# Low parts of the turned attention tiles taken by VectorE out of the transposes' bank

## What is computed

```
q, k = partial_rope(rmsnorm(q, q_gain)), partial_rope(rmsnorm(k, k_gain))   # two maps per head, 64 wide
s = einsum('mbhqd,mbhkd->mbhqk', q_blk, k) / sqrt(64)
p = softmax(s);  a = p[0] - lam * p[1]                # 8 heads, 4 blocks of 128 queries
o = einsum('bhqk,bhkv->bhqv', a, v)                   # v 128 wide
o = rmsnorm(o, sub_gain) * (1 - lambda_init)
x = x + o @ w_o
```

## Time and profile before

| | |
|---|---|
| median of 3 runs | 1055.51 us (1054.57 to 1055.61) |
| span of the profiled execution | 1052.2 us, first to last instruction |
| what lies around the span | 3.3 us, if the profiled execution took the median |
| TensorE busy | 1010.8 us, 96% |
| VectorE busy | 603.8 us, 57% |
| ScalarE busy | 410.5 us, 39% |
| GpSimd busy | 278.8 us, 26% |
| mean granted TensorE clock | 0.994 of full speed |

### The profile page before, as it was taken

The page is one execution under the profiler, slowest core; times in us unless marked ns, Lnnn a source line. Parts: engine busy times, 40 slices in busy tenths (PEclk is TensorE's granted clock), DMA queues, the critical chain, the costliest instruction groups (busy, mean ns, idle before and its releaser), DMA issues.

```text
span 1052.2 us, 13519 instructions
## 1 busy us (share of the span) xinstructions
PE 1010.8 (96%) x4812; PEld 826.8 (79%) x4812; DVE 603.8 (57%) x867; ACT 410.5 (39%) x659; POOL 278.8 (26%) x330
## 2 busy tenths in 40 slices
PE   6999998889899999999999999999999999999998
PEld 5877876666678788888888888878888888888886
DVE  5667989877957554544445444676444444454442
ACT  4535555577645241222422314553324223142231
POOL 5852678566547850000000000650000000000000
PEclk9999999999999999999999999999999999999999
DMA  6422111120222232323223322213233233332302
GB/s 241 144 44 98 60 41 60 61 81 1 80 82 80 88 98 96 100 88 112 93 86 100 100 90 70 79 62 121 95 105 100 80 101 98 100 100 80 114 6 80
DMA packets 46899, 92.38 MB, mean 88 GB/s; under 512 B 8848, under 2 KB 13968, under 8 KB 46864
## 3 DMA queue, kind: packets, MB, share of 16 engines
q1 hardware_dynamic: 40768, 91.24, 26.3%
q10 hardware_dynamic: 6096, 0.69, 0.5%
HBM read 89.82 MB, written 2.10 MB: 87 GB/s over the span
## 4 chain that ended last, share of the span: by engine, by line
PE 77%; DVE 10%; POOL 6%; issue 4%; ACT 1%; DMA 1%; ACTq 0%; POOLq 0%; SPq 0%; DVEq 0%
PE bank L1198 75%; DVE s_nmax L1004 2%; PE bank L1256 1%; POOL s_nsum L607 1%; DVE s_qkn L956 1%; DVE s_p L1026 1%; POOL s_w_lo L651 1%; DVE s_w_lo L913 1%; POOL s_oc L585 1%; DVE s_mixc L1024 1%; DVE s_rt L960 1%; POOL s_o_r L582 1%; DVE s_qk_ss L943 1%; DMA s_raw<-in_attn_w_qkv 1%; POOL s_qk_r L552 1%
## 5 line engine op out<-in xcount | busy, mean ns | idle before, releaser
L670 ACT ACTIVATE s_w_hi<-s_raw 128x1024 fp32r<-128x1024 f32 (+1 forms) x164 | 164.8, 1039 | 229.4 <-PE bank L1198 226.4
L913 DVE TENSOR_TENSOR s_w_lo<-s_raw,s_w_hi 128x1024 fp32r<-128x1024 f32 (+1 forms) x160 | 198.3, 1242 | 26.4 <-ACT s_w_hi L670 26.2
L1198 PE MATMUL bank<-s_hT_hi,s_w_hi 128*128 128x512 f32 x512 | 201.0, 393 | 0.9 <-DVE s_hT_lo L1091 0.8
L1198 PE MATMUL bank<-s_uT_hi,s_w_hi 128*128 128x512 f32 x512 | 199.7, 390 | 0.5 <-DVE s_uT_lo L1126 0.5
L1198 PE MATMUL bank<-s_hT_hi,s_w_lo 128*128 128x512 f32 x512 | 199.3, 389 | 0.0
L1198 PE MATMUL bank<-s_hT_lo,s_w_hi 128*128 128x512 f32 x512 | 199.3, 389 | 0.0
L1198 PE MATMUL bank<-s_uT_hi,s_w_lo 128*128 128x512 f32 x512 | 199.2, 389 | 0.0
L1198 PE MATMUL bank<-s_uT_lo,s_w_hi 128*128 128x512 f32 x512 | 199.2, 389 | 0.0
L1074 DVE TENSOR_TENSOR s_xT<-s_xT,bank 128x512 f32<-128x512 f32 x128 | 87.5, 688 | 158.6 <-PE bank L1198 158.6
L831 ACT ACTIVATE s_uT_hi<-s_z 128x512 fp32r<-128x512 f32 x64 | 40.5, 632 | 221.4 <-DVE s_z L1121 221.4
L1198 PEld LDWEIGHTS bank<-s_hT_hi,s_w_hi 128*128 128x128 f32 x512 | 96.1, 188 | 23.1 <-DVE s_hT_lo L1091 3.0
(11 more groups left out here) (151 smaller groups left out, 1314.0 us busy)
## 6 DMA issues: line engine op xcount, KB each, us to landing
s_raw<-in_mlp_w SPq DMA_DIRECT2D x128, 512.0 KB, 3.4
s_raw<-in_attn_w_qkv SPq DMA_DIRECT2D x24, 512.0 KB, 3.8
s_raw<-in_attn_w_o SPq DMA_DIRECT2D x8, 512.0 KB, 3.2
s_x_nat<-in_x SPq DMA_DIRECT2D x4, 512.0 KB, 8.2
s_x_again<-in_x SPq DMA_DIRECT2D x4, 512.0 KB, 5.2
out<-s_onat SPq DMA_DIRECT2D x8, 256.0 KB, 2.4
s_raw<-in_pool_w SPq DMA_DIRECT2D x4, 256.0 KB, 2.7
s_g_bc<-in_norm_mix ACTq DMA_DIRECT2D x1, 512.0 KB, 5.4
```

Source lines behind the costliest of these rows:

```text
L670: a.activation(w_hi[slot][:, k * width:(k + 1) * width], raw[k][:, 0:width], ACT.Copy)\
L913: v.tensor_tensor(w_lo[slot][:, cols], raw[k][:, 0:width], f32(w_hi[slot][:, cols]), ALU.subtract)\
L1198: return nc.tensor.matmul(o, lhsT, rhs, start=start, stop=stop, **kw)
```

## The change

VectorE takes the low part of every turned tile straight out of bank 4, as (bank x scale) - high. ScalarE's second copy, the scratch tile and GpSimd's subtraction are gone. The signal `turn_kept` now follows the first copy, and TensorE waits for `turn_lo_done` of the turn before it writes bank 4 again. On VectorE the low part of a map stands behind `combine(i-1)` in step i, that of an extra turn at the head of the next step, and those of q and k of head 0 behind the v low parts of tiles 9 and 10.

```diff
-                pool.wait_ge(turn_kept, k + 1)
-                g.tensor_tensor(lo, turn_raw[:, k % 2, :], f32(hi), ALU.subtract).then_inc(turn_lo_done, 1)
...
-            turn_lo("q", 0)
-            turn_lo("k", 0)
             for i in range(LAST + 1):
-                if i - 1 in EXTRA:
-                    turn_lo(*EXTRA[i - 1])
...
-                if 2 <= i < STEPS + 2:
-                    turn_lo("map", i - 2)
...
-                a.activation(hi, bank[4][:], ACT.Copy, scale=scale)
-                if k >= 2:
-                    act.wait_ge(turn_lo_done, k - 1)
-                a.activation(turn_raw[:, k % 2, :], bank[4][:], ACT.Copy, scale=scale).then_inc(turn_kept, 1)
+                a.activation(hi, bank[4][:], ACT.Copy, scale=turn_scale(what)).then_inc(turn_kept, 1)
...
+            def turn_lo(what, n):
+
+                k = TURN_NO[what, n]
+                hi, lo = turn_dst(what, n)
+                dve.wait_ge(turn_kept, k + 1)
+                if what == "map":
+                    last = v.tensor_tensor(lo, bank[4][:], f32(hi), ALU.subtract)
+                else:
+                    last = v.scalar_tensor_tensor(lo, bank[4][:], turn_scale(what), f32(hi), ALU.mult, ALU.subtract)
+                last.then_inc(turn_lo_done, 1)
...
                         v_lo_part(0, t, bank[n % 4])
+                    if n == 2 * NT + 1:
+                        turn_lo("q", 0)
+                    if n == 2 * NT + 2:
+                        turn_lo("k", 0)
...
             for i in range(LAST + 1):
+                if i - 1 in EXTRA:
+                    turn_lo(*EXTRA[i - 1])
...
                 if 1 <= i <= STEPS:
                     combine(i - 1)
+                if 2 <= i < STEPS + 2:
+                    turn_lo("map", i - 2)
...
                 if k:
-                    pe.wait_ge(turn_kept, k)
+                    pe.wait_ge(turn_lo_done, k)
...
-            pe.wait_ge(turn_kept, len(TURNS))
+            pe.wait_ge(turn_lo_done, len(TURNS))
```

More of the change, by code:

```diff
@@ L200, in build_trunk @@
                                     ("band_lo", [P, NG, NT, BW], F32R))
-        aT_hi, aT_lo, p0, p1, turn_raw, oc, osq, qkT1_hi, qkT1_lo = inside(
+        aT_hi, aT_lo, p0, p1, oc, osq, qkT1_hi, qkT1_lo = inside(
             scratch, ("aT_hi", [P, 2, S], F32R), ("aT_lo", [P, 2, S], F32R),
-            ("p0", [P, 2, S], F32), ("p1", [P, 2, S], F32), ("turn_raw", [P, 2, S], F32),
+            ("p0", [P, 2, S], F32), ("p1", [P, 2, S], F32),
             ("oc", [P, 2, S], F32), ("osq", [P, S], F32),
@@ L370, in turn_dst, with turn_scale @@
             return qkT_hi[n % 2][:, "qk".index(what), :], qkT_lo[n % 2][:, "qk".index(what), :]
+        def turn_scale(what):
+            if what == "map":
+                return 1.0
+            if what == "o":
+                return sub_col[:, 0:1]
+            return qk_col[:, 0:1] if what == "q" else qk_col[:, 1:2]
         def piece(slab, k):
@@ L553, in qk_root @@
                     .then_inc(qk_r_done, 1)
-            def turn_lo(what, n):
-                k = TURN_NO[what, n]
-                hi, lo = turn_dst(what, n)
-                pool.wait_ge(turn_kept, k + 1)
-                g.tensor_tensor(lo, turn_raw[:, k % 2, :], f32(hi), ALU.subtract).then_inc(turn_lo_done, 1)
             qk_square(0)
@@ L717, in keep_turn @@
                 act.wait_ge(turned, k + 1)
-                scale = 1.0
                 if what == "map":
@@ L721, in keep_turn @@
                         act.wait_ge(pv_done, n - 1)
[L722 to L727, removed]
-                a.activation(hi, bank[4][:], ACT.Copy, scale=scale)
-                if k >= 2:
-                    act.wait_ge(turn_lo_done, k - 1)
-                a.activation(turn_raw[:, k % 2, :], bank[4][:], ACT.Copy, scale=scale).then_inc(turn_kept, 1)
+                elif what in "qk" and n >= 2:
+                    act.wait_ge(scored, NT * (n - 1))
+                a.activation(hi, bank[4][:], ACT.Copy, scale=turn_scale(what)).then_inc(turn_kept, 1)
             act.wait_ge(rope_reduced, 1)
```

## The result

The changed kernel takes 1069.99 us in the median (1068.18 to 1072.12, 4 runs) against 1055.56 us: a ratio of 1.0132, 95% interval 1.0118 to 1.0146. It is slower by some 14 us, where the prediction had +7.0 (1062.5) and a range that ended at 1070: the result lies at its very edge. The direction was right, the size off by a factor of two. Executions of one kernel differ by up to 7 us, with the granted clock; all comparisons of times are of medians, and what a trace shows is one execution. The span of the profiled execution is 1066.4 us, 14.2 more than before.

What follows compares the result with a forecast made beforehand. VectorE nearly full in a first regime, waits between engines inside each step in a second; +2.1 (start) - 3.5 (first) + 8.4 (second and end) = +7.0 on 1055.51 gives 1062.5 us, range 1054 to 1070.

Steps and rivals of the forecast that it cites:

- Relief and work in the first regime: Steps 5 to 16, VectorE nearly full: 20 us returned against 13.2 added, net -6.8, of which -3.5 lands.
- the relief: VectorE time returned in the first regime when GpSimd's subtractions no longer stretch its operations: 20 us.
- the bounds of -6.8 and +1: First regime: -6.8 us if all lands, +1 if GpSimd's squares and roots stretch VectorE instead.
- The start: Turn of k0 waits for q0's low part on VectorE, starting at 82.25 us instead of 80.16: +2.1 us.
- the upper bound (+3.7): Largest loss allowed at the start, with a clock drop included: +3.7 us.
- The second regime: Later attention steps and end, neither engine full: lengthened steps less returns give +8.4 us, bounds +4 and +12.
- the turn-free steps: Steps 19, 29, 30 and 31, without an extra turn: each returns 0.5 us, 2.0 in all.
- The loop: Steps with an extra turn: the turn waits behind maxima and mix, 3.13 + 2.44 = 5.57 us against 4.25.
- Relief wins: Rival, chance 0.17: all -6.8 us land and the second regime costs only +2; faster, 1052.8 us.
- my mark of 4.6 us: Loop length in steps with an extra turn; measuring under about 4.6 us decides for relief wins.
- cancel: Rival, chance 0.13: losses and relief nearly balance, +0.6 us, 1056.1 us, within 0.2% of before.
- The clock falls more often: Rival, chance 0.11: TensorE's new idle waits bring two or three more clock drops, +4 us on the forecast, 1067 us.

Runs made afterwards that it cites:

- scratch_vector: Changed kernel, but ScalarE again makes its second copy into a scratch tile, which frees bank 4, and VectorE subtracts from that tile; 1047.01 us.
- short_pool_low: The kernel before the change, with GpSimd's 56 subtractions cut to 8 of 512 columns; 1034.83 us.
- warm_waits: Changed kernel with unread products keeping TensorE busy ahead of the turn of k0 and eight extra turns (those of q, k or o); 1065.78 us.
- short_vector_low: Changed kernel with VectorE's 56 subtractions cut to 8 of 512 columns, every wait and order kept; 1049.4 us.
- low_before_mix: Changed kernel with the map's low part moved on VectorE to between maxima(i) and the mix of i-1; 1056.58 us.
- both_orders: Changed kernel with the map's low part between maxima and mix, and q0's low part right behind the norms of tile 7; 1047.09 us.
- start_early: Changed kernel with the low part of q0 put right behind the norms of tile 7 on VectorE; 1066.54 us.

## Why the prediction was half the size

**Relief and work in the first regime: -3.5 predicted, -3.4 measured.** The number came right partly by luck. The stretching of VectorE by GpSimd was read rightly (the mix now takes 752 ns), as were the two prices of the new subtraction. Steps 5 to 16 by their reciprocals, in the kernel before, the changed one, scratch_vector and short_pool_low (VectorE's busy time is the third after the length):

```profile
120.30:210.30 90.00, 79.31 (x440) 62.45 (x439) 81.90 (x149) 53.71 (x108) 61.43 (x45) 0.96 0.14 49
124.70:211.30 86.60, 77.72 (x438) 60.67 (x437) 77.39 (x170) 42.87 (x85) 31.02 (x23) 0.98 0.16 51
120.70:202.20 81.50, 76.24 (x440) 60.29 (x439) 77.37 (x171) 53.44 (x107) 31.76 (x24) 1.00 0.16 55
119.80:196.20 76.40, 75.82 (x440) 60.29 (x439) 65.96 (x149) 53.41 (x107) 36.15 (x45) 1.00 0.17 56
```

VectorE's busy time fell by 4.5 us and not by 6.8: the relief is 16 to 18 us (15.9 in short_pool_low; 4.5 and the 13.2 of added work here), where I had booked 20. What such a net is worth in time is another matter. scratch_vector has the same 77.4 us on VectorE and its regime is 8.5 us shorter than before. Up to 3.4 of these are two stretches at half clock that the kernel before has here and scratch_vector has not. The changed kernel is 5.1 us longer than scratch_vector, by the bank wait and by one drop at 162.3 us (up to 1.7). I had no price for the wait in this regime. And my -3.5, called half way between the bounds of -6.8 and +1, is about half of the one bound; half way is -2.9.

**The start: +2.1 predicted, +4.4 measured.** The turn came 2.6 us later; 0.4 us of that was there before anything that the change touches (the turn of q0 starts at 72.83 against 72.48). Of the rest, 1.6 us are the drop to half clock at 83.8 us, directly behind an idle time of 3.86 us: from the turn of k0 to scores(0) it takes 7.63 us, against 6.06 before and 6.00 in warm_waits, where the drop is gone. I had written it down as the upper bound (+3.7) and left it out of the sum.

**The second regime: +8.4 predicted, +14.6 measured.** This is the step that failed: the sum of the lengthened steps took every step at full clock and took a return from the turn-free steps that did not come. The loop itself was right: 3.21 us to the turn against 3.13, 5.65 us in all against 5.57, and steps 17, 25, 27 and 28 take 5.64, 5.65, 4.77 and 7.39 us (forecast: 1.3 above 4.2, 5.57, 4.8, and 1.3 above 5.9). Three things are missing. First, the drops of the clock in steps 20, 21 and 24: these steps take 7.85, 7.16 and 8.66 us, and 7.20, 5.60 and 7.25 in warm_waits, so the drops cost at least 3.6 us. Second, the turn-free steps 19, 29, 30 and 31 gave back 0.8 us and not 2.0: what the mix no longer loses, the new subtraction takes, since in this regime too VectorE is on the path of each step. short_vector_low shows the latter. Third, GpSimd's scaling of o (line 583) stretches the mix of step 20 inside the loop, by 0.67 us:

```profile
228.17 1.42 DVE L1029 SCALAR_TENSOR_TENSOR s_p<-s_p,s_mixc 128x512 f32<-128x512 f32 x1
```

And from the recorded end of a low part to the turn it takes 0.14 us (237.37 to 237.52) and not 0.06. The stretched mix and the 0.14 us are read from the trace, not tried. Against all this, step 18 took 0.8 us less than its share of the forecast.

**The rivals.** *Relief wins* was refuted for this change, but what the relief does to the time was underestimated: removing GpSimd's subtractions is worth 21 us of the kernel's time, and a version without the bank wait is faster than before. What decided was the point that I had named, the length of the loop: 5.65 us here, 4.50 in low_before_mix. By my mark of 4.6 us that kernel should have been faster than before, and it ties with it, the size of *cancel*: its start is some 6 us longer. With the start mended as well (both_orders) it is 0.9% faster. *The clock falls more often* was wrong in its name: five times against four. But the drops that follow the new waits lie on the path, and their cost should have been a part of the forecast and not a rival: the forecast made idle times of up to 2.7 and 3.7 us, and the trace of before had shown at 189.44 what can follow such a time.

What I had not seen is that wait and work cost more together than apart (35 us against 12 + 15). I priced the work where VectorE is full and the wait where it is not, and each exists in both.

## What to carry to other kernels

When work is moved to another engine together with the right to free a shared buffer, price the two apart: who does the work, and behind what in its queue the release now stands. Here the same 56 subtractions on VectorE make the kernel 0.8% faster through a scratch tile and 1.3% slower out of the bank, and moving one operation ahead of another in the queue is worth 13 us. If a forecast makes new idle time on TensorE in front of work on the path, the lower clock behind it belongs in the sum. Count first the drops that the kernel already has: here it had four, and the fifth and the new places of the others made the difference.

## What was unexpected of the hardware

GpSimd's 56 subtractions, of 1.29 us in the median, cost the kernel 21 us although the others waited little for them (TensorE 0.7 us, its weight loads 1.9, ScalarE 2.1). Beside GpSimd's work even a VectorE operation on 128x1 elements (line 1024) took up to 1253 ns against 207. Behind idle times of TensorE of 3.86, 2.82, 2.66 and 2.00 us the clock stood at half for 3.4 us, and in other kernels for up to 13.7 us in one piece (start_early, from 226.5 us). In the kernel before it also fell behind waits of only 1.34 us (at 219.7 us) and 1.08 us (at 281.1). And 14 (or 5 to 10) products that nobody reads, put into the waits, kept it up in four places and made the kernel faster by 4 us.
